# A two-block transformer kernel: norm parts built beside the residual, and linears placed inside the attention stages

## What is computed

```python
for l in range(2):                                   # block 1
    h = rms_norm(x, norm_mix[l])
    x = x + (even_mixer if l == 0 else odd_mixer)(h, ...)
    x = x + memory_cross_attention(rms_norm(x, norm_cross[l]), rms_norm(mem, norm_mem[l]), ...)
    x = x + conv_ffn(rms_norm(x, norm_ffn[l]), ffn_w_up[l], ffn_conv_w[l], ffn_conv_b[l], ffn_w_down[l])
for l in range(2):                                   # block 2
    x = x + 0.5 * swiglu(rms_norm(x, ffn1_norm[l]), ...)
    x = x + hybrid_mixer(rms_norm(x, mix_norm[l]), positions, ...)
    x = x + memory_cross_attention_2(rms_norm(x, ca_norm[l]), rms_norm(mem_2, mem_norm[l]), ...)
    x = x + 0.5 * swiglu(rms_norm(x, ffn2_norm[l]), ...)
out = rms_norm(x, final_norm)
```

## Time and profile before

| | |
|---|---|
| median of 3 runs | 2695.26 us (2693.7 to 2696.86) |
| profiled execution, span | 2693.7 us |
| TensorE busy | 2426.5 us, 90% |
| VectorE busy | 1680.1 us, 62% |
| ScalarE busy | 1115.9 us, 41% |
| mean granted TensorE clock | 0.918 |

### The profile page before, as it was taken

One profiled execution on the slowest core, in us unless ns is written; L12 is line 12 of the kernel. 1 busy time (PEld: TensorE's weight loads), 2 busy tenths in 40 slices (PEclk: granted clock), 3 DMA queues, 4 the chain that ended last, 5 costly groups with the idle time before them and its releaser, 6 DMA issues.

```text
span 2693.7 us, 40616 instructions
## 1 busy us (share of the span) xinstructions
PE 2426.5 (90%) x17557; PEld 2237.8 (83%) x17557; DVE 1680.1 (62%) x2336; ACT 1115.9 (41%) x1314; POOL 31.5 (1%) x53
## 2 busy tenths in 40 slices
PE   6877899997688998999998789999999998789998
PEld 6747799994578998999984578999999994578997
DVE  4465587755467877666446767666666445767664
ACT  4334454433355444334342354334334253345332
POOL 0103000000000000000000000000000000000000
PEclk8878999997799999999996789999999997789998
DMA  7525245450124554555540234554555640043552
GB/s 217 142 26 143 94 158 187 158 189 16 63 94 143 188 188 141 188 181 156 158 136 1 68 126 140 186 176 164 179 188 158 168 149 16 28 160 109 179 188 79
DMA packets 322821, 365.40 MB, mean 136 GB/s; under 512 B 24495, under 2 KB 298691, under 8 KB 322515
## 3 DMA queue, kind: packets, MB, share of 16 engines
q1 hardware_dynamic: 316723, 349.12, 39.8%
q0 software_dynamic: 4336, 7.31, 1.7%
q10 hardware_dynamic: 1584, 6.36, 0.6%
HBM read 357.78 MB, written 4.98 MB: 135 GB/s over the span
## 4 chain that ended last, share of the span: by engine, by line
PE 76%; DVE 14%; ACT 8%; issue 2%; DVEq 0%; DMA 0%; ACTq 0%; PEldq 0%
PE bank L630 22%; PE bank L633 21%; PE bank L631 21%; DVE wlo L1223 3%; PE bank L781 2%; PE bank L828 2%; ACT xs_hi L989 2%; DVE wk L1296 2%; ACT whi L937 2%; PE bank L717 1%; PE bank L817 1%; ACT wk L991 1%; PE bank L705 1%; PE bank L783 1%; PE bank L725 1%
## 5 line engine op out<-in xcount | busy, mean ns | idle before, releaser
L630 PE MATMUL bank<-xs_hi,wlo 128*128 128x256 f32 x3920 | 1013.5, 293 | 94.9 <-DVE xs_lo L1293 42.8
L631 PE MATMUL bank<-xs_lo,whi 128*128 128x256 f32 x3920 | 994.8, 289 | 0.0
L937 ACT ACTIVATE whi<-raw 128x2048 fp32r<-128x2048 f32 (+2 forms) x344 | 638.7, 1860 | 836.9 <-PE bank L633 814.5
L1223 DVE TENSOR_TENSOR wlo<-raw,whi 128x2048 fp32r<-128x2048 f32 (+2 forms) x344 | 761.5, 2224 | 237.9 <-ACT whi L937 237.7
L630 PEld LDWEIGHTS bank<-xs_hi,wlo 128*128 128x128 f32 x3920 | 771.3, 197 | 116.6 <-issue 94.9
L631 PEld LDWEIGHTS bank<-xs_lo,whi 128*128 128x128 f32 x3920 | 775.9, 198 | 0.3
L633 PE MATMUL bank<-xs_hi,whi 128*128 128x256 f32 (+1 forms) x3920 | 572.3, 287 | 0.0
L633 PEld LDWEIGHTS bank<-xs_hi,whi 128*128 128x128 f32 (+1 forms) x3920 | 520.9, 196 | 4.3
L630 PE MATMUL bank<-act_hi,wlo 128*128 128x256 f32 x1056 | 276.4, 283 | 5.4 <-DVE wlo L1223 5.4
L631 PE MATMUL bank<-act_lo,whi 128*128 128x256 f32 x1056 | 276.3, 283 | 0.0
L633 PE MATMUL bank<-act_hi,whi 128*128 128x256 f32 x1056 | 212.9, 283 | 0.0
(11 more groups left out here) (205 smaller groups left out, 2057.9 us busy)
## 6 DMA issues: line engine op xcount, KB each, us to landing
raw<-in_ffn_w_gu SPq DMA_DIRECT2D x88, 1024.0 KB, 5.1
raw<-in_ffn_w_down SPq DMA_DIRECT2D x66, 1024.0 KB, 5.3
raw<-in_ffn_w_up SPq DMA_DIRECT2D x44, 1024.0 KB, 5.1
raw<-in_w_in SPq DMA_DIRECT2D x42, 1024.0 KB, 5.2
raw<-in_ca_w_kv SPq DMA_DIRECT2D x16, 1024.0 KB, 5.0
raw<-in_od_w_in SPq DMA_DIRECT2D x12, 1024.0 KB, 5.1
raw<-in_ev_w_in SPq DMA_DIRECT2D x10, 1024.0 KB, 5.3
raw<-in_w_in SPq DMA_DIRECT2D x20, 512.0 KB, 5.0
```

The lines of the kernel that those rows point to most:

```text
L630: eng.matmul(out, a[1], b[0], start=first and i == 0, stop=False, skip_group_check=True)
L631: eng.matmul(out, a[0], b[1], start=False, stop=False, skip_group_check=True)
L937: eng.activation(whi[i % SETS][:, 0:ch["n"]], raw[i % SLOTS][:, 0:ch["n"]], ACT.Copy).then_inc(S["weights_hi"], 1)
L1223: eng.tensor_tensor(wlo[i % SETS][:, 0:n], raw[i % SLOTS][:, 0:n], whi[i % SETS][:, 0:n].bitcast(F32), ALU.subtract)\
```

## The change

**No barrier to the next linear.** Stages carry `join`; a stage with `join=True` has no drain and no wait for the other engines. The linears that follow a norm (mixer inputs, q and k) and the FFNs are joined. The other stages keep their barrier, and TensorE may now emit linear units between its drain and the wait (the "pre" slot).

**Norm parts with the residual.** `norm_pair` and `norm_lo` make the high and low parts of two tiles of the next norm as soon as these tiles of `xT` have had their last addition, inside the stage that adds. They are written to the other of two pairs of buffers (`X[0]`, `X[1]`). The sum of squares is eight float32 matmuls per norm (`sum_pair`, two per pair of tiles) where there was one, and the reduction on VectorE (L1296) is gone. `as_it_comes` runs the first two units of a linear side by side, two tiles at a time, with the sums in between.

**Linears inside attentions.** `enroll` gives numbers to units that no linear stage owns; each heads, index or attention stage has a table `fill`: at iteration i, TensorE emits units up to one number, ScalarE and VectorE split the weights up to two chunks beyond at the beginning of that iteration and empty the bank of the unit before. Moved in this way are 8 input units and 4 output units of half size in the even mixer, 6 and 4 in the odd one, the two v units of each cross attention, and the twelve gate units of each hybrid mixer. Softmax attentions now have two score banks, the dual ones one turn bank and one result bank, since the `lin_bank`s are in use. Output projections of block 1's mixers are cut in two by rows, so that the first half can run before the second attention is done. The tanh of gates is put off to the end of attention stages (`flush`), and the scaling went into the multiplication that uses them.

**Memory norms once.** `mem` and `mem_2` are turned and normed with both layers' gains inside the first linear of each block, stored to memory, and read back as a chunk by each cross attention (`mem_chunk`). The `enter`, `tables` and `split` stages are gone: their work is in a `start` stage and in linears. The branch projections are read in pieces of 128 rows, nine loads for each pair of chunks.

```diff
+        def mem_chunk(layer, buf, last_unit):
+
+
+            c = len(chunks)
+            chunks.append({"pieces": [(raw[c % SLOTS][:, :], mem_in[layer].ap())], "n": CHUNK, "mem": buf, "layer": layer,
+                           "last": last_unit})
 
...
+        def enroll(units):
...
+            for un in units:
+                un["u"] = number("lin")
+                un["taker"], un["taken"] = ("lin_moved", number("plain") + 1) if un["post"] == "plain" else ("lin_free", number("taken") + 1)
...
+                chunks[un["chunk"]]["release"] = ("lin_ready", un["u"] + 1)
+                units_of.append(un)
+            return [un["u"] for un in units]
...
+            linear(units, norm=norm, join=True, tokens=True, spread=True, mem=dict(which=0, at=(1, 3)), first=True)
             g = prow["ev_attn_qk_gain"]
+
+            M = features(w, b, 768, 512, 6) + features(w, b, 1280, 512, 10, scale=P ** -0.5)
+            M = enroll(M + values(w, b, 1792, 512, 128) + features(w, b, 2304, 512, 14, "sigmoid"))
+            for u in M[2:4]:
+                units_of[u]["after"] = ("t5_stored", 16 * 4)
             heads_norm([(0, 2, g), (2, 2, g), (4, 2, g + 1)], HD, "rows_even", "axial",
+                       dict(cell=True, n=number("gates"), width=16, bias=gate_bias[:, 0:16]),
+                       fill={"pre": (M[1], M[0]), 0: (M[2], M[1]), 1: (M[3], M[2])}, mem_scale=0)
+            attention("softmax", [small_head(o, 0, 4, h, (h // 4) * HD, h, kh=h // 4, bias=None) for h in range(8)],
+                      fill={0: (M[4], M[3]), 2: (M[5], M[4]), 4: (M[6], M[5]), 6: (M[6] + 1, M[6]), 8: (M[6] + 1, M[6] + 1)})
+            H = enroll(residual_half(wo, o, 0))
             attention("mlstm", [head(ft[:, 6 + h, :], ft[:, 10 + h, :], 0, P, vt[:, :, 128 + h * P:128 + (h + 1) * P],
+                                     ft[:, 18 + h, :], h=h) for h in range(4)],
+                      fill={0: (H[0], M[7]), 1: (H[1], H[0]), 3: (H[2], H[1])}, tanh=M[7] + 1)
+            heads_norm([(18 + h, 1, prow["ev_mlstm_gain"] + h) for h in range(4)], P, "rows_cell",
+                       fill={"pre": (H[3], H[2]), 0: (H[3] + 1, H[3]), 1: (H[3] + 1, H[3] + 1)})
+            parts = make_parts(ft[:, 18:22, :], 4, o, 4, by=ft[:, 14:18, :], scale=0.5)
+            return linear(residual_half(wo, o, 1), parts=parts, then=then)[-1]
...
-        def cross_attention(l, gain, mem_gain, wq, wkv, wo, qk_gain):
-            norm_first(xT, gain)
-            linear(features(wq, 0, 512, 0, scale=1.0 if qk_gain is not None else P ** -0.5))
-            norm_first(memT, mem_gain)
-            linear(features(wkv, 0, 512, 4) + values(wkv, 512, 512, 0))
+                                          ft[:, 16 + h, :], bias=t5_bias[:, h]) for h in range(4)], fill={1: (H[3], H[2])})
+            heads_norm([(16 + h, 1, prow["od_diff_gain"] + h) for h in range(4)], P, "rows_diff",
+                       fill={"pre": (H[3] + 1, H[3]), 0: (H[3] + 1, H[3] + 1)})
+            parts = make_parts(ft[:, 16:20, :], 4, o, 4)
+            return linear(residual_half(wo, o, 1), parts=parts, then=then)[-1]
+
+        def cross_attention(norm, then, layer, before, wq, wkv, wo, qk_gain):
+            b, o = norm["buf"], 1 - norm["buf"]
+            units = features(wq, b, 0, 512, 0, scale=1.0 if qk_gain is not None else P ** -0.5)
+            mem_chunk(layer, o, before)
+            units += features(wkv, o, 0, 512, 4, "plain")
+            linear(units, norm=norm, join=True)
+            V = enroll(values(wkv, o, 512, 512, 0, "plain"))
+            fill = {"pre": (V[1], V[0]), 0: (V[1] + 1, V[1]), 1: (V[1] + 1, V[1] + 1)}
             if qk_gain is not None:
-                heads_norm([(0, 2, qk_gain), (2, 2, qk_gain), (4, 2, qk_gain + 1), (6, 2, qk_gain + 1)], P, "rows_cross")
-            attention("softmax", [head(ft[:, h, :], ft[:, 4 + h, :], 0, P, vt[:, :, h * P:(h + 1) * P], out_tile(h, 0, P), bias=None)
-                                  for h in range(4)])
-            units = []
-            for half in range(2):
-                c, v, [tiles] = row_chunk([wo], half * 512, 512)
-                units += [feature_unit(c, v, 0, tiles, i * SEQ, 2, "residual", 4 * half + 2 * i) for i in range(2)]
-            linear(units)
-
-        def ffn(gain, w_up, w_down, scale, conv_layer):
-
-            norm_first(xT, gain)
+                heads_norm([(0, 2, qk_gain), (2, 2, qk_gain), (4, 2, qk_gain + 1), (6, 2, qk_gain + 1)], P, "rows_cross", fill=fill)
+            attention("softmax", [head(ft[:, h, :], ft[:, 4 + h, :], 0, P, vt[:, :, h * P:(h + 1) * P], out_tile(b, h, 0, P), bias=None)
+                                  for h in range(4)], fill=None if qk_gain is not None else fill, values_in=(units_of[V[1]]["taker"], units_of[V[1]]["taken"]))
+            linear(residual_half(wo, b, 0), then=then)
...
+            linear(units, norm=norm, join=True, tokens=True, mem=dict(which=1, at=(3, 6)) if l == 0 else None, angle=l == 0)
+            G = enroll(features(w, b, 3662, 3 * D, 0, "sigmoid", dst=gt))
+            for u in G[4:]:
+                units_of[u]["after"] = ("mem_stored", 16 * 2 * DEPTH)
             heads_norm([(t, n, None) for t, n in ((3, 2), (5, 1), (12, 2), (14, 1), (18, 2), (20, 2), (22, 1))], rope="full",
+                       gates=dict(cell=False, n=number("gates"), width=6, bias=gate_bias[:, 16 + 6 * l:22 + 6 * l]),
+                       fill={"pre": (G[1], G[0]), 0: (G[2], G[1])})
+            stage("index", u0=number("idx", 8), fill={"pre": (G[3], G[2])})
+            attention("softmax", [small_head(o, 0, 9, h, h * HD, h, bias=C3("causal"), row=h, top_k=True, causal=True) for h in range(6)],
+                      fill={0: (G[4], G[3]), 2: (G[5], G[4]), 4: (G[6], G[5]), 6: (G[7], G[6])}, tanh=G[5])
+            attention("softmax", [small_head(o, 3, 12, h, 384 + h * HD, 6 + h, bias=other[0][0], causal=True) for h in range(5)],
+                      fill={0: (G[8], G[7]), 2: (G[9], G[8]), 4: (G[10], G[9])}, tanh=G[8])
+            attention("stick", [small_head(o, 6, 15, h, 704 + h * HD, 11 + h, causal=True) for h in range(5)],
+                      fill={0: (G[11], G[10]), 2: (G[11] + 1, G[11]), 4: (G[11] + 1, G[11] + 1)})
...
-            def enter(i):
-                if i:
-                    eng.wait_ge(S["act_stage"], i)
-                    eng.wait_ge(S["dve_stage"], i)
+            def enter(i, st):
+
+                if i and not st["join"]:
+                    eng.drain().then_inc(S["pe_stage"], 1)
+                    if st.get("after"):
+                        eng.wait_ge(S["att_done"], st["after"])
+                    fill(st, "pre")
+                    eng.wait_ge(S["act_stage"], st["bar"])
+                    eng.wait_ge(S["dve_stage"], st["bar"])
                 if i == more_consts_at:
                     eng.wait_ge(S["more_consts_loaded"], 16)
...
+            def sum_pair(nm, p):
+
+                eng.wait_ge(S["sq_ready"], 4 * nm["n"] + p + 1)
+                for i in range(2):
+                    m = eng.matmul(post_bank[1][:, 0:SEQ], C("add128"), squares[p][:, i * SEQ:(i + 1) * SEQ],
+                                   start=p == 0 and i == 0, stop=p == 3 and i == 1, skip_group_check=True)
+                if p == 3:
+                    m.then_inc(S["ss_ready"], 1)
+
+            def as_it_comes(pairs, signal, at, per, nm=None):
+
+
+                n = len(pairs[0][1][0][1])
+                for k0 in range(0, n, per):
+                    if nm is not None and k0 + per == n:
+                        sum_pair(nm, 3)
+                    eng.wait_ge(S[signal], at + k0 + per)
+                    for bank, mms, chunk_of, before in pairs:
+                        if k0 == 0:
+                            arrived(chunk_of)
+                            before()
+                        for i, (o, operands) in enumerate(mms):
+                            for k in range(k0, k0 + per):
+                                a, b = operands[k]
+                                eng.matmul(bank[:, o], a[1], b[0], start=i == 0 and k == 0, stop=False, skip_group_check=True)
+                                eng.matmul(bank[:, o], a[0], b[1], start=False, stop=False, skip_group_check=True)
+                            for k in range(n if k0 + per == n else 0):
+                                a, b = operands[n - 1 - k]
+                                m = eng.matmul(bank[:, o], a[0], b[0], start=False, stop=k == n - 1, skip_group_check=True)
+                        if k0 + per == n:
+                            yield m
+                    if nm is not None and k0 + per < n:
+                        sum_pair(nm, k0 // per)
...
+            def fill(st, slot):
+
+                if slot in st["fill"]:
+                    while emitted[0] < st["fill"][slot][0]:
+                        unit(emitted[0])
...
+            def fill(st, slot):
+
+                if slot in st["fill"]:
```

(22 more changed lines are left out.)

1039 lines of the change are left out of this document (618 added, 421 removed).

## The result

The changed kernel takes **2589.3 us** (median of 4 runs, 2586.5 to 2595.2) where the kernel before took 2695.0 (4 runs beside it): 0.9614 of the time, 95% interval 0.9600 to 0.9629. The gain is 106 us. The forecast was 2473 us, a gain of 222. The sign was right, but less than half of the forecast gain came. The question of the rest of this text is which of the forecast's terms failed and why.

The account below looks back on a forecast made before the run. TensorE's stream, busy 90% of the span, was taken to bound the kernel. Gains of 134 + 34 + 25 + 2 + 9 + 9 + 9 = 222 us took 2,693.7 to 2,471.7, given as 2,473 us; range 2,390 to 2,590, own range 2,425 to 2,525.

Parts of the forecast that it names:

- Linears inside attentions: Eight attention regions: 50 moved units interleaved, 681 us where serial work would take 814.5; gain 134 us.
- chains between engines, no full engine: Mixer regions from heads to last heads: clock 0.66 to 0.72, VectorE and ScalarE at most two thirds busy.
- Queues in series, the second rival: Attentions: in-order VectorE and ScalarE queues make each moved unit delay its stage in full; 134 us gone, 2,607 us; chance 0.19.
- Norms 34 us: Thirteen norms of x: 91 us lost before, 57 after, with parts made beside TensorE's output products; gain 34 us.
- mixer outputs 9: Mixer output linears: two thirds of 3.3 us over 23.0 go, warmer clock and no first wait; gain 9 us.
- splits 9: The four `split` stages, taken as 20 us, shrink to the first tile's parts; gain 9 us.
- start 2: Program start: first product at about 15 instead of 31.2 us, with work moved into the first linear; gain 2 us.
- the parts keep up: Norms of x: ScalarE's three 0.59 us instructions a pair fit TensorE's 16 products, 1.9 us, a pair.
- memory norms 25: Cross attentions' k and v linears: the memory norm's 6.3 us go, four times; gain 25 us.
- gates 9: Hybrid mixers' 24 gate units, every 6.15 us instead of 5.76, no longer set the pace; gain 9 us.
- rival "slower": Filled attention stages stay at half clock, 225 us more on top of queues in series: 2,832 us; chance 0.03.
- turning point: Where the change turns slower: 229 us over the sum, all queue delays and 21 of 50 units at half clock.

Follow-up runs that it names:

- e1: Changed kernel with every moved linear unit taken out of the attention stages and put in a row ahead of them; 2651.2 us.
- e5: Changed kernel with three orders changed: additions and low parts first in output linears, split ahead of rotations in hybrid heads, gate tanhs one by one in projections; 2562.7 us.
- e3: Changed kernel with moved units' weight splits and emptyings at the end of each attention iteration on ScalarE and VectorE, behind the head's own work; 2627.6 us.
- e2: Changed kernel with six of the eight float32 matmuls of each norm's sum of squares left out; 2558.5 us.
- e14: Changed kernel with earlier reorderings and GpSimd adding squares, plus next weights' high part ahead of tile parts in output linears, first weight load after x; 2508.1 us.
- e9: Changed kernel with five order changes together (hybrid heads, tanhs, moved units in halves, output linears, memory load at the start), no work left out; 2554.9 us.
- e11: Changed kernel with the products of the moved units cut to their first k tile, splits, waits and emptyings kept; 2506.5 us.
- e13: Changed kernel with moved units' products cut to their first k tile and their weight splits cut to 64 columns; 2425.4 us.

## Why the forecast was wrong

**Linears inside attentions, 134 us: the step that failed most.** Measured 62 us by e1, 76 us by the windows against the earlier trace rows. The forecast gave the regions 681 us: TensorE's work of 570 at full clock, and 111 for chains and barriers. The work was right (566). Idle time came out at 101, so the allowance for chains was right in size too. What the sum left out is half clock: TensorE lost 71 us to it inside the regions after the change, and that is more than the 57 us by which they exceed 681.

The misreading stands ahead of the sum: "chains between engines, no full engine". That is true of a whole region in the earlier trace rows, not of its stages. In the fox stage of the kernel before TensorE was busy for 34.31 of 37.90 us at clock 0.55, and in e1 it is busy 87 to 92% of the eight-head and fox stages, without a moved unit in them. There was little idle time to fill; there was slow time. In the eight softmax and stick-breaking stages of the mixers 25 units were moved (144 us by count). From e1 to the kernel after these stages grew by 102 us, 71% of those 144: 150 us more work at full clock, 42 less lost to half clock, and only 6 less idle, of 49. The rows of the even mixer's eight-head stage, in e1 and in the kernel after, show what such a stage is like:

```profile
133.70:162.00 28.30, 25.11 (x112) 15.47 (x111) 16.75 (x44) 12.82 (x42) 21.46 (x35) 0.82 0.50 139
98.40:147.80 49.40, 47.51 (x304) 38.90 (x303) 29.51 (x57) 20.42 (x46) 21.77 (x35) 0.93 0.62 182
```

I had put it at 46 us as TensorE's, and TensorE's it is, 47.51 of 49.40; (1 - 0.93) x 47.51 makes 3.3 of the 3.4 us that it is longer. By stages the 57 us are 28 in the heads stages ahead of attentions (15 of them the three-way wait that e5 removed, 6 the odd mixer's second heads), 12 in the mLSTM and differential stages and 18 in the others, less 1 in the cross attentions. The waits for queues and rings are in there, as idle time and, by way of the clock, once more as lost time: e5's order of the heads took away 5.4 us of idle in a hybrid mixer's heads stage and 7.9 us of its length. Why the clock falls where it falls in the filled stages is open.

**Queues in series, the second rival, 2607 us.** Nearer to the result than the forecast, and VectorE did wait 86 us more for high parts. But the mechanism that it named, a split ahead of a head's maximum, did not pay when it was removed: in e3, with the split behind, the kernel took 38 us more. The waits that did cost were rings: one in the hybrid heads (15 us for both mixers), one in the output linears. That the rival's time is only 18 us from the result is mostly luck: it had every moved unit delay its stage in full, and they did so by 71%. My reason against the rival, that the split is two chunks ahead and its inputs are there, was right for the data and wrong for the queue: the high part was late because ScalarE stood for something else.
The Trainium skill's rule that I set against the trace (TensorE: Matmul & The Clock Gate, table of specs: ScalarE and VectorE strictly in order) made this rival the likelier one. The trace agrees with the rule at 1292.14, where VectorE stood 11.51 us with ready work behind.

**Norms 34 us, mixer outputs 9, splits 9, start 2.** The remainder of the change gave 43 us of 88. The sums cost what I charged (e2), and at the end of an FFN the term held (0.89 us of waiting, I allowed 1). At the end of output linears I assumed that "the parts keep up" because ScalarE needs three instructions of 0.59 us a pair. I counted one engine's load and not the ring with VectorE and the weights: 25 us, if what e14 gave in these stages (13.4 for the two hybrid mixers, 11.3 for the six others) is taken as what the ring had cost. The projections, whose tanhs I had left at 0, took 6.4 and 5.3 us more than in the kernel before (38.6 and 37.4 for 32.2 and 32.0); the tanhs' order gave 6 of these back in e5 and 9 with the others in e9. The gain of 9 for the split stages counted 8 us twice, since the region windows of 111.8 and 105.7 already ended behind the first mixers' split stages. The start lost 6 us instead of gaining 2: the first stage took 60.6 us, and 100.9 less its eight moved units is 54.8. The first product came 7 us later than forecast, since x arrived some 5 us later than before; but with x back in its place (e14) the stage was no shorter, so the cause of this loss is not shown. These make 12 + 25 + 8 + 8 = 53, more than the 45 missing, so either the other terms (memory norms 25, gates 9) came out better than forecast or these prices overlap. They were not measured by themselves.

**A slip in the sum of the rival "slower".** Its turning point is at the whole gain, 222 us over the sum, not at 229; nothing hangs on it.

**What held.** TensorE's work in the regions (566 us for 570), TensorE as the bound, the cross attentions (36, 36, 23, 23 against 35.2, 34.4, 23.9, 23.9), the wait behind an FFN, the sums, the stored t5 rows being there in time (the even mixer's heads stage is 37.8 against 36), and that neither half clock nor late tiles made the kernel slower than before, though half clock took a good part of the gain.

**What stays open.** In the differential stage TensorE is busy for 20.33 of 36.60 us; the stage took 36.5 to 40.8 us in every kernel here, longest where products were thin, and no run took its chain apart. The mLSTM stage's 3 us between kernels that share its code go with the granted clock (0.74 and 0.84); why that differed is not known. No run changes the clock by itself, so its price here is read from the traces and not from an edit.

## What to carry to other kernels

When work is put into the gaps of a chain, first look at each stage by itself, with three numbers beside each other: length, busy time of the bounding engine, granted clock. Idle time can be filled; time at half clock can't, it only shrinks if the clock rises. Here 49 us of idle and 72 us of half-clock loss in eight stages gave back 6 and 42 when 144 us of work were put in. Do not count the filled stage at full clock unless a row shows that it gets it. Follow each new instruction once round the engines: if engine A's step waits for B and B's next step stands behind something that waits for A, the sum of the ring is the period, and only an edit that takes one step out of the ring helps. Price a moved unit by leaving out its parts one at a time and together, and split each price into idle time and clock: a part that is left out can come back as either.

## What was unexpected of the hardware

A GpSimd addition of 128 x 4096 took 9.04 us where VectorE needs 4.43, and held back VectorE's two-input instructions for all of it (11.35 us for 2.74). Twenty-six additions of 128 x 512, 1.36 us each, also slowed VectorE's low parts (580 ns each on average for 481), but saved 19.6 us in all. In the fox stage 115 TensorE records took 40.78 us at granted clock 0.54 (e11) and 116 of them 35.54 at 0.66 (e13), with the same idle time: what looked like the price of splits there was the clock. At the start, x 5 us earlier did not make the first stage shorter.
